# A hybrid decoder layer with 32 experts: rows gathered already transposed, gate-and-up weights loaded in 4 MB pairs, a shorter routing stage

## The reference, cut to what matters

```python
logits = x2 @ router_w + router_b
top_vals, top_idx = lax.top_k(logits, 4)
gates = softmax(top_vals)
# for each expert e, the rows of the tokens that chose it:
gu = xb @ w_gu[e] + b_gu[e]                 # (1024 x 2048) weights
gate = minimum(gu[:, :1024], 7.0); up = clip(gu[:, 1024:], -7.0, 7.0)
h = (up + 1.0) * (gate * sigmoid(1.702 * gate))
y = h @ w_down[e] + b_down[e]               # (1024 x 1024) weights
```

## Time and profile before

| what | value |
|---|---|
| runs shown | 1216.87 us median of 3 (1216.04 to 1221.18) |
| profiled execution | 1217.71 us, of it 1215.9 us span |
| PE busy | 1156.7 us (95%), 5736 matmul records |
| DVE, ACT busy | 513.6 us (42%), 254.9 us (21%) |
| DMA | 443.69 MB, mean 365 GB/s over the span, 428 GB/s from 320 us on |
| granted TensorE clock | 0.992 of full speed |

### The profile page before, as it was taken

How to read it: one execution, slowest core, us unless ns; L and a number is a source line. 1 busy time by engine, 2 the same in 40 slices (tenths; PEclk the granted TensorE clock), 3 DMA queues, 4 the chain that set the end, 5 groups by cost and what they waited for, 6 DMA issues and landing times.

```text
span 1215.9 us, 14046 instructions
## 1 busy us (share of the span) xinstructions
PE 1156.7 (95%) x5736; PEld 562.1 (46%) x5736; DVE 513.6 (42%) x977; ACT 254.9 (21%) x398; POOL 3.2 (0%) x12
## 2 busy tenths in 40 slices
PE   9999999999999999999999998999999999999994
PEld 8989999654333333333333323333333333333331
DVE  4888878663333232223332222323222222222236
ACT  4645565311111111111111111111111111111112
POOL 1000000000000000000000000000000000000000
PEclk9999999999999999999999999999999999999998
DMA  9756754646999999999999999999999999999993
GB/s 234 237 168 206 230 146 143 263 179 258 408 430 428 425 429 428 428 426 426 430 427 425 429 427 427 429 427 426 428 428 427 427 428 428 426 427 429 427 424 154
DMA packets 93399, 443.69 MB, mean 365 GB/s; under 512 B 7848, under 2 KB 65336, under 8 KB 67998
## 3 DMA queue, kind: packets, MB, share of 16 engines
q1 hardware_dynamic: 93246, 442.67, 89.8%
q10 hardware_dynamic: 96, 0.22, 0.0%
HBM read 441.34 MB, written 1.53 MB: 364 GB/s over the span
## 4 chain that ended last, share of the span: by engine, by line
PE 57%; DMA 29%; DVE 10%; issue 2%; ACT 2%; DVEq 0%; SPq 0%; ACTq 0%
DMA ring<-in_w_gu 24%; PE PS L821 20%; PE PS L854 13%; PE PS L734 6%; PE PS L649 5%; DMA ring<-in_w_down 3%; PE PS L756 3%; PE PS L667 2%; DVE w_lo L960 2%; DVE tiles L998 2%; DVE tiles L1062 1%; PE PS L742 1%; PE PS L790 1%; PE PS L749 1%; PE PS L894 1%
## 5 line engine op out<-in xcount | busy, mean ns | idle before, releaser
L821 PE MATMUL PS<-ring,mid 128*64 128x512 f32 x1920 | 424.6, 596 | 24.5 <-DMA ring<-in_w_gu 24.5
L821 PEld LDWEIGHTS PS<-ring,mid 128*64 128x64 f32 x1920 | 135.6, 137 | 307.4 <-issue 256.2
L854 PE MATMUL PS<-ring,mid 128*64 128x512 f32 x960 | 212.6, 595 | 0.0
L1261 DVE TENSOR_SCALAR PS<-PS 128x512 f32<-128x512 f32 x30 | 21.0, 700 | 368.5 <-PE PS L821 368.5
L649 PE MATMUL PS<-x_hi,w_hi 128*128 128x320 f32 x448 | 142.4, 318 | 3.9 <-DVE w_lo L960 3.9
L649 PE MATMUL PS<-x_hi,w_lo 128*128 128x320 f32 x448 | 139.7, 312 | 0.0
L649 PE MATMUL PS<-x_lo,w_hi 128*128 128x320 f32 x448 | 139.7, 312 | 0.0
L1243 DVE TENSOR_TENSOR ys<-PS,ys 64x512 fp32r<-64x512 f32 x64 | 44.1, 689 | 200.7 <-ACT ys L567 190.8
L854 PEld LDWEIGHTS PS<-ring,mid 128*64 128x64 f32 x960 | 66.3, 137 | 130.8 <-issue 130.8
L998 DVE SCALAR_TENSOR_TENSOR x_tok<-PS,gate,x_tok 128x1024 f32<-128x1024 f32 (+1 forms) x93 | 115.1, 1276 | 19.7 <-PE PS L756 19.7
L558 ACT ACTIVATE mid<-PS 128x512 f32<-128x512 f32 x30 | 17.9, 597 | 434.2 <-DVE PS L1261 434.2
(11 more groups left out here) (225 smaller groups left out, 731.1 us busy)
## 6 DMA issues: line engine op xcount, KB each, us to landing
ring<-in_w_gu SPq DMA_DIRECT2D x124, 2048.0 KB, 40.0
ring<-in_w_down SPq DMA_DIRECT2D x62, 2048.0 KB, 38.9
raw<-in_w_in SPq DMA_DIRECT2D x56, 512.0 KB, 5.1
ring<-in_w_gu SPq DMA_DIRECT2D x8, 1024.0 KB, 7.4
ring<-in_w_out SPq DMA_DIRECT2D x4, 1024.0 KB, 6.1
ring<-in_w_down SPq DMA_DIRECT2D x4, 1024.0 KB, 41.6
x_tok<-in_x_prompt SPq DMA_DIRECT2D x1, 1024.0 KB, 6.2
out<-x SPq DMA_DIRECT2D x2, 512.0 KB, 2.7
```

What stands on the lines that cost most here:

```text
L821: last = mm(PS[64 * a:64 * a + 64, b, :], xgT[:, 2 * (u % 2) + j, u // 2, :], w[:, o:o + HALF], start=False, stop=(u == 3 and j == 1))
L854: last = mm(PS[64 * a:64 * a + 64, XB, :], hT[:, j, u, :], w[:, j * D + a * HALF:j * D + (a + 1) * HALF], start=(u == 0 and j == 0), stop= ...
L1261: dve.tensor_scalar(gm, gm, LIMIT, None, ALU.min).then_inc(gm_ok, 1)
```

## The change

1. The gather is turned round: the tokens `x1` are the stationary operand (every fourth column of a half, 128 of them), the one-hot the moving one (64 columns). The result is `xgT` at once. It is 24 matmuls in place of 6; `turn_x` and one of ACT's two copies go.
2. `w_gu` is loaded in pairs of slots, 4 MB with 32 KB in a partition, for units 6 to 9 and from unit 18 on; a pair's load waits until PE has done with both old units, and PE waits for the whole pair. Units 12 to 15 stay single. Unit 6, which was loaded before unit 5, now comes with unit 7 after the first layer norm.
3. Routing: the bias is added by a matmul, logits are handed over tile by tile, `match_replace` and a comparison make the mask in place of `max_index` and one-hot comparisons, the ranks come from 3 fp32r matmuls (and 3 for the counts) in place of 9 fp32 ones, and the gates are computed after the first one-hot. The transposes of positions and gates (`turn_tables`) move between units 1 and 2 of expert 0, and its bias sums between its down matmuls. At the start DVE makes fp32r copies of two constants.
4. In the last expert the sums for expert 30 come one half unit later.

```diff
@@ SP
+                    v = u // 2
+                    return 4, w_gu[0, e, 4 * v * P:4 * (v + 1) * P, :].rearrange("a (p j) n -> p (a j) n", j=4)
...
+                elif is_gu(n):
+                    sp.dma_start(ring[:, s:s + 2, :].rearrange("p s n -> p (s n)").rearrange("p (j n) -> p j n", j=k),
+                                 src).then_inc(gu_in[s // 2], 16)
...
             for n in range(SLOTS, UNITS * (LOOP + 2)):
-                sp.wait_ge(used, n - SLOTS + 1)
+                together = is_gu(n) and n >= SINGLE
+                if together and n % 2:
+                    continue
+                sp.wait_ge(used, n + together - SLOTS + 1)
                 load_unit(n)
@@ PE, gather
-                for t, (t0, n) in enumerate(TILES):
-                    for a in range(2):
-                        last = mm(PS[64 * a:64 * a + 64, XB, :], onehot[0:n, t, :],
-                                  x1[0:n, t, a * HALF:(a + 1) * HALF], start=(t == 0), stop=(t == 2))
-                last.then_inc(xg_done, 1)
...
+                        for a in range(2):
+                            first, o = a * HALF + 2 * v + j, ((2 * v + j) * 2 + a) * ROWS
+                            for t, (t0, n) in enumerate(TILES):
+                                last = mm(PS[:, XB, o:o + ROWS], x1[0:n, t, first:first + 4 * P - 3:4],
+                                          onehot[0:n, t, :], start=(t == 0), stop=(t == 2))
+                last.then_inc(xg_done, 1)
@@ PE, one_expert
                 if i + 1 < NE:
                     if i + 1 not in ALONE:
                         add_bias(1 - s)
-                    pe.wait_ge(xg_ok, 2 * it + (rows_in(i) + 1))
-                    pe.wait_ge(hT_ok, 2 * it + (i + 1))
-                    turn_x(xg_sb, tx_done)
-                pe.wait_ge(c_taken, 6 * it + (3 * i + 1))
-                sum_up(0)
+                    pe.wait_ge(xgT_ok, 2 * it + (rows_in(i) + 1))
+                if i > 0:
+                    pe.wait_ge(c_taken, 6 * it + (3 * i + 1))
+                    sum_up(0)
@@ DVE, routing, for each tile as its logits arrive
+                link(dve.tensor_copy(lg[0:n, t, 0:NE], PS[0:n, LG_BANK[t], t * NE:(t + 1) * NE]))
+                link(dve.max(top[:, t, :], lg[:, t, 0:NE]))
+                dve.tensor_scalar(ek[:, t, :], lg[:, t, 0:NE], top[:, t, 0:1], None, ALU.subtract).then_inc(top_ok, 1)
+                link(dve.memset(top[:, t, TOPK:], LOWEST))
+                link(dve.match_replace(left[:, t, :], top[:, t, :], lg[:, t, :], HIGHEST))
+                last = dve.tensor_tensor(mask[:, t, :], left[:, t, 0:NE], lg[:, t, 0:NE], ALU.is_gt)
```

More of the change, by code:

```diff
@@ L24 @@
 PB = 4
-SLOTS, UNITS = 10, 6
+SLOTS, UNITS, SINGLE = 10, 6, 16
 WIDE = 4 * D
@@ L221, in route @@
             return x_tok[:, 2, rat[0] - n:rat[0]]
-        lg = route(96).rearrange("p (t e) -> p t e", t=3)
-        mask = route(96).rearrange("p (t e) -> p t e", t=3)
-        cnt, ext, incl, excl = (route(32) for _ in range(4))
+        lg = route(120).rearrange("p (t e) -> p t e", t=3)
+        left = route(120).rearrange("p (t e) -> p t e", t=3)
+        route(96)
+        mask = place("mask", [P, 3, NE], XT + 8 * D + 4 * (rat[0] - 96), F32R)
+        mask_f = mask[:, :, :].bitcast(F32)
+        ext, incl, excl = (route(32) for _ in range(3))
         top = route(24).rearrange("p (t k) -> p t k", t=3)
-        idx = route(24).bitcast(U32).rearrange("p (t k) -> p t k", t=3)
-        idf = route(24).rearrange("p (t k) -> p t k", t=3)
-        ek = route(12).rearrange("p (t k) -> p t k", t=3)
+        ek = route(96).rearrange("p (t e) -> p t e", t=3)
         es = route(3)
@@ L293, in placed, with is_gu @@
             return (NE - 2 + n // 4, n % 4) if n < 8 else (NE - 2 + (n - 8) // 2, 4 + n % 2)
+        def is_gu(n):
+            return placed(n)[1] < 4
         def landed(n, it):
-            twice = 2 if (n - UNITS * LOOP) % SLOTS < 2 else 1
-            return it * (16 * twice) + 16 * (n // SLOTS + 1 + (n % SLOTS < 4))
+            a, b = UNITS * LOOP, UNITS * (LOOP + 2)
+            if is_gu(n):
+                same = [m for m in range(0, UNITS * NE, 2) if is_gu(m) and m // 2 % 5 == n // 2 % 5]
+                parts = [4 if m < 4 else 2 if SLOTS < m < SINGLE else 1 for m in same if m <= n]
+            else:
+                same = [m for m in range(UNITS * NE) if not is_gu(m) and m % SLOTS == n % SLOTS]
+                parts = [1 for m in same if m <= n]
+            count = sum(parts)
+            return it * 16 + 16 * count if n >= a and any(a <= m < b for m in same) else 16 * count
         def rows_in(i):
@@ L402, in _ @@
                             j = UNITS * s + u
-                            before = j - SLOTS if j >= SLOTS else j - 2 * UNITS if j >= 2 * UNITS - SLOTS else j - 2
+                            if is_gu(u) and u % 2:
+                                continue
+                            last = j + is_gu(u)
+                            before = last - (SLOTS if last >= SLOTS else 2 * UNITS if last > 1 else 2)
                             sp.wait_ge(used, it * (2 * UNITS) + (UNITS * LOOP + before + 1))
@@ L611, in _, with keep_warm @@
             mm = pe.matmul
+            def keep_warm(n, bank):
+                for _ in range(n):
+                    mm(PS[:, bank, :], ones_r[:, :], bias4[:, 0, :], start=True, stop=True)
             def keep_busy(n, bank):
@@ L931, in _ @@
                     last = down(w, hT_last, u, (2 * half, 2 * half + 1), 1)
-                    if u == 0 and half == 0:
+                    if u == 0 and half == 1:
                         pe.wait_ge(ylo_ok, twice + i)
@@ L1155, in _ @@
-            dve.wait_ge(top_ok, 1)
-            for t in range(3):
-                last = dve.tensor_tensor(oh4[:, t], iota[:, 0:NE].unsqueeze(1).to_broadcast([P, TOPK, NE]),
-                                         idf[:, t, 0:TOPK].unsqueeze(2).to_broadcast([P, TOPK, NE]), ALU.is_equal)
-            link(last)
-            link(dve.tensor_reduce(mask, oh4.rearrange("p t k e -> p t e k"), AX_X, ALU.add))
-            dve.memset(mask[NS:P, 2, :], 0.0).then_inc(mask_ok, 1)
-            dve.wait_ge(exp_ok, 1)
@@ L1171, in _ @@
-            dve.memset(gate[NS:P, 2, :], 0.0).then_inc(gate_ok, 1)
-            dve.wait_ge(gate_ok, 1)
+            for q, t in enumerate(T_ORDER):
+                n = TILES[t][1]
+                dve.wait_ge(lg_done, q + 1)
+                link(dve.tensor_copy(lg[0:n, t, 0:NE], PS[0:n, LG_BANK[t], t * NE:(t + 1) * NE]))
[4 more added lines that the diff above has]
+                last = dve.tensor_tensor(mask[:, t, :], left[:, t, 0:NE], lg[:, t, 0:NE], ALU.is_gt)
+                if t == 2:
+                    link(last)
+                    link(dve.memset(mask_f[NS:P, 2, :], 0.0))
```

233 lines of the change are left out of this document (120 added, 113 removed).

## The result

The changed kernel takes 1580.9 us, median of 4 runs (1579.3 to 1581.9), against 1216.9 us for the kernel before on the same chip: 1.298 times as long, 95% interval 1.295 to 1.301. The prediction was 1253.5 us, slower by 3.0%. The side was right, the size was far off: 327 us above the forecast, and outside the range.

What follows compares the result with a forecast made beforehand. PE, no longer the weight stream, was to bound the kernel: 285.4 + 31.0 + 29 x 29.5 (855.5) + 9.2 + 22.6 + 48.8 = 1252.5 us of span, so 1253.5 us, 3.0% slower; range 1228 to 1275 us.

Steps and rivals of the forecast that it cites:

- The bound: Whole kernel: before, the DMA weight stream at 428 GB/s sets the end; after the change, PE does.
- The free room of 1.1 us an expert: PE's 33 us of waiting for weights, over 29 experts; growth beyond 1.1 us each makes PE set the end.
- a record costs 0.113 to 0.12 us: Turned gather on PE: weight loads pace its 48 records, so it takes 5.65 us, where it took 2.87.
- The third rival: Gather: strided fp32 loads last 0.208 us, gather 10 us, end near 1380 us, or 1315 at half the excess; chance 0.08.
- the signs that I named for a wrong forecast: Record spacing under 0.09 us, PE waiting for `w_gu` as before, or a DMA rate so low that PE waits again.
- the tail: Start of expert 31 to the end of the span: 48.8 us in place of 49.85.
- Routing: Routing stage before expert 0: the gather starts near 278.8 us, 5.3 us earlier; gate and up at 285.4 in place of 289.87.
- The pairs: Paired `w_gu` loads: a wait of up to 3.5 us against maybe 1% faster stream; both costed at nothing.
- What PE gets back without `turn_x`: Each expert on PE: of `turn_x`'s 0.47 us only 0.32 us returns; ACT's lost copy brings nothing.
- the copies at the start: DVE's copies of constants before its first wait for data: cost nothing, otherwise 0.4 us.
- the later sums of expert 30: Last expert: sums moved by half a unit save the 0.5 us in which PE waited for DVE's `ys`.
- The rule for loads: Gather: a load takes columns / 1.2 ns; by it alone 48 loads take 5.1 us and the end is 16 us earlier.

Runs made afterwards that it cites:

- run 6: Changed kernel with w_gu laid out in the ring as before the change (gather step 2) and gather matmuls ordered by row count; 1304.1 us, ratio 1.070.
- run 1: Changed kernel with the gather of before, its four transposes and ACT's second copy back; 1212.0 us, ratio 0.995 to the kernel before.
- run 5: Changed kernel with the gather's token columns side by side (step 1) and its matmuls ordered by row count, outputs not the layer's; 1283.2 us, ratio 1.053.
- runs 11: The kernel of run 1 measured again, unchanged; 1214.5 us, ratio 0.9982 to the kernel before.
- run 2: Changed kernel with the gather's token columns side by side (step 1), order of matmuls kept, outputs not the layer's; 1429.8 us, ratio 1.172.

## Why the prediction was wrong in size

- **The bound** was read rightly. The free room of 1.1 us an expert, beyond which PE and not the stream sets the end, gives the sign: run 6, with 2.5 us more on PE even where the full clock holds (29.54 against 27.02), is slower, and run 1, with the old gather, is not.
- **The gather, "a record costs 0.113 to 0.12 us", is the step that failed.** At the full clock it costs 0.11 for weights side by side, 0.23 at the step of 4, and 0.15 more at each of 15 changes of the row count. I took L749's strided transposes for a twin, since "the step is the same". Its 0.12 us came from three records in one window, and it holds between the last three of the four transposes in the other experts too. It shows that a strided *transpose* can follow the one before by 0.12 us; it did not show it for these fp32 matmuls, and they need 0.23. And none of the rows that I priced from mixes row counts inside a stream, so they could not hold the second cost, nor did any of my rivals.
- **The third rival** ("the step costs more on fp32 weights than on transposes") named the right mechanism, the step, and got a chance of 0.08. Its gather of 10 us was short, as it lacked the changing rows (2.4 us) and the clock; 1380 us in place of 1580. Of the signs that I named for a wrong forecast none lies on this side: all are of records that follow too fast or of PE waiting for weights.
- **The clock** stood in no term. The clock was 1.00 in every row of before, and the sum let all else run on at that pace. In the expert shown, the changed kernel pays 1.7 us for it behind the gather (4.45 - 2.73) and 0.5 us in `down` (7.42 against 6.92).
- **Summed:** the span is 326.3 us longer than forecast. The start of gate and up of expert 0 is 294.77 in place of 285.4, 9.4 us (8.3 in the gather, 1.1 behind it, where I had 0.9 us for waits, copy and bias and it took 2.0); from there to expert 30 it is 1203.4 in place of 895.7, 307.7 us; expert 30 is 31.9 in place of 22.6, 9.3 us; the tail is 48.8 as forecast:

```profile
1498.16 13.90 PE L920 MATMUL PS<-ring,mid 128*64 128x512 f32 x64
...
1530.04 3.22 PE L920 MATMUL PS<-ring,mid 128*64 128x512 f32 x14
```

Of the 307.7 us, expert 0 has 12.5 (43.5 in place of 31.0) and expert 15 with the gather behind the loop 19.7 (58.4 in place of 38.7; that gather takes 14.3 us at a mean clock of 0.53). The other 28 have 9.8 each; the one shown is 10.3 over the 29.5: 8.2 in the gather, 2.2 by the clock. By the runs: putting the rows together gives 62.7 us back (1580.9 to 1518.2), and side by side loads give 235 us on top (1518.2 to 1283.2). In the other order they give 151 (1580.9 to 1429.8) and then 147 (1429.8 to 1283.2): the two costs can't be added up one by one, since most of the clock returns only when both are gone (mean clock 0.848, then 0.849 or 0.895 with one gone, 0.964 with both). 30 us are left over the forecast. Of these, 21 are the 1.3 us of low clock in 16 experts of run 5, some 4 the gather behind its loop (9.4 us at a clock of 0.57 in place of 5.6), and 3 the later start of expert 0 (288.4 in place of 285.4).
- **Routing** was right to half a microsecond, and the exact hit is luck. The gather began at 278.8 as forecast, where it was 284.10:

```profile
277.14 0.31 PE L752 MATMUL PS<-mask,upper_r 128*128 128x96 f32 x1
...
278.78 14.06 PE L770 MATMUL PS<-onehot,x 128*128 128x64 f32 x48
...
294.77 8.20 PE L855 MATMUL PS<-ring,mid 128*64 128x512 f32 x32
```

But 0.5 us of the 5.3 is an earlier start of the stage. From the first logits to the first gather it is 10.63 us, where it was 15.42 (268.68 to 284.10): 4.8 us saved. It is 10.63 in the other runs too, while the time at which the stage began lay anywhere from 267.2 to 272.2 in these profiles. With the old gather kept (run 1) the first gate and up begins at 283.5, 6.4 us before; the end comes 3 to 5 us earlier (runs 11 and 1), as the stream is the bound there.
- **The pairs** cost nothing here, as forecast, since PE waits for no weights. **What PE gets back without `turn_x`** fits run 5: where its clock held, it is 2.78 us from the gather to `down`, 2.73 by my sum, and 29.3 us for the expert, where 27.02 - 2.87 + 5.53 - 0.32 is 29.4. The tail came as forecast; the copies at the start and the later sums of expert 30 were not tried alone.
- **The rule for loads.** I cited the Trainium skill (TensorE: Matmul & The Clock Gate, LDWEIGHTS) for columns / 1.2 ns, whatever the partitions: 5.1 us for 48 loads. It fits loads side by side (0.11 us, 128 or 64 rows alike). The section says nothing of a step, and 48 loads at the step of 4 took 11.4 us.

## What to carry to other kernels

Before moving a tensor to the stationary side, look at its distance between elements: for these fp32 matmuls a step of 2 was nearly free (0.12 us a load against 0.11) and a step of 4 doubled every load (0.23). Keep matmuls of one row count together, which one accumulation group over the whole bank allows, and don't price a stream of loads from a neighbour of another kind, but from records of the same form, step and order. And a long stretch of loads with few moving columns had a second bill here, since the clock fell in it or behind it. Cutting it in two with wide matmuls between gave 16 us back, and none of these versions came down to the 1217 us of the kernel before.

## What was not expected of the hardware

- A change of the row count between 128 and 64 in a stream of weight loads takes about 0.15 us at the full clock (0.26 against 0.11 at step 1). At the granted clock of 0.50 it is 0.45 us where the rows change (418.76 to 419.21) and 0.21 where they don't (below).
- The load at the step of 4 keeps its pace at both clocks: 12 loads and 11 in windows of 3 us at 1.00 and 0.50 (above), and 0.23 us from load to load of one form at either. So it is not the array's clock that paces it. Loads side by side go from 0.11 to 0.21 us, as these of run 2 at 0.50 show:

```profile
418.76 0.33 PEld L770 LDWEIGHTS PS<-onehot,x 64*128 64x128 f32 x1
...
419.21 0.29 PEld L770 LDWEIGHTS PS<-onehot,x 128*128 128x128 f32 x1
...
419.38 0.33 PEld L770 LDWEIGHTS PS<-onehot,x 128*128 128x128 f32 x1
419.59 0.33 PEld L770 LDWEIGHTS PS<-onehot,x 128*128 128x128 f32 x1
```

- The clock fell while PE was busy for 100% of the time. In the changed kernel it fell 34 times, and 32 of the falls began 2.4 to 5.7 us after the start of a gather, among its loads with 64 moving columns each (of the others one came 1.0 us into the gather behind the loop, after PE had been idle, and one in the tail). With 512 moving columns in the gather (run 1) it fell 5 times, never within 15 us of a gather's start, and the mean clock of the span was 0.988, against 0.848.
- What stays open: why the transposes of h, with the same step of 4, follow each other at 0.12 us and the gather's loads at 0.23 (a transpose is one record, a gather matmul two; not tried), why a change of the row count costs what it does, whether 32 KB runs bring 0.5%, and what moves the start of the routing stage by up to 5 us from one profile to the next.
